# Three norms and the weight blocks behind them, joined without a barrier, in a two-layer diffusion step on one core

## The reference, cut to what matters

```python
for l in range(DEPTH):
    sh1, sc1, gt1, sh2, sc2, gt2 = modulation(cond, w_mod[l], b_mod[l])     # silu(cond) @ w_mod + b_mod
    h = rmsnorm(x, g_pre_mix[l]) * (1.0 + sc1) + sh1
    o = mix(h, ...)                     # u = h @ w_in, attention and RWKV-7, then @ w_o
    x = x + gt1 * rmsnorm(o, g_post_mix[l])
    h = rmsnorm(x, g_pre_ffn[l]) * (1.0 + sc2) + sh2
    f = swiglu(h, w1, w3, w2)           # l == 0; l == 1: top-2 of 8 experts
    x = x + gt2 * rmsnorm(f, g_post_ffn[l])
```

## Time and profile before

| | |
|---|---|
| time, 3 runs | 2856.21 us median (2851.51 to 2856.57) |
| the profiled execution | 2857.58 us, of which span 2855.8 us |
| PE busy | 2631.8 us (92%) |
| DVE busy | 1336.7 us (47%) |
| ACT busy | 1055.3 us (37%) |
| POOL busy | 172.0 us (6%) |
| mean granted clock of TensorE | 0.967 of full |

### The profile page before, as it was taken

How to read it: one execution, slowest core, us unless ns; L and a number is a source line. 1 busy time by engine, 2 the same in 40 slices (tenths; PEclk the granted TensorE clock), 3 DMA queues, 4 the chain that set the end, 5 groups by cost and what they waited for, 6 DMA issues and landing times.

```text
span 2855.8 us, 63857 instructions
## 1 busy us (share of the span) xinstructions
PE 2631.8 (92%) x28250; PEld 2263.3 (79%) x28250; DVE 1336.7 (47%) x2420; ACT 1055.3 (37%) x1993; POOL 172.0 (6%) x175
## 2 busy tenths in 40 slices
PE   5998799997999999999997999979799999999995
PEld 3996588785799994449964878957799999999994
DVE  2237445556422320023464455663456555655565
ACT  3225443444412110023254444442444444444442
POOL 0002011110000000010010111100100000000010
PEclk8999899998999999999998999998899999999998
DMA  6223023300122221121200330001556665666571
GB/s 254 79 76 120 24 99 121 112 12 5 67 74 75 81 74 59 60 77 62 79 18 1 120 103 21 4 5 60 202 186 203 210 211 177 214 207 208 184 263 56
DMA packets 82683, 304.31 MB, mean 107 GB/s; under 512 B 9376, under 2 KB 9504, under 8 KB 82272
## 3 DMA queue, kind: packets, MB, share of 16 engines
q1 hardware_dynamic: 71072, 257.93, 26.4%
q0 software_dynamic: 11328, 42.21, 4.0%
HBM read 273.10 MB, written 27.00 MB: 105 GB/s over the span
## 4 chain that ended last, share of the span: by engine, by line
PE 85%; DVE 9%; ACT 2%; issue 2%; DMA 1%; POOL 0%; DVEq 0%; SPq 0%; PEldq 0%; POOLq 0%; ACTq 0%
PE ps L416 17%; PE ps L417 17%; PE ps L418 17%; PE ps L1303 7%; PE ps L1094 6%; PE ps L1102 3%; PE ps L429 2%; PE ps L744 2%; PE ps L830 2%; PE ps L873 1%; PE ps L1005 1%; PE ps L889 1%; DVE arena L2165 1%; DVE arena L2164 1%; DMA ring<-in_blocks 1%
## 5 line engine op out<-in xcount | busy, mean ns | idle before, releaser
L1987 DVE TENSOR_TENSOR ring_lo<-ring,w_ffn 128x1024 fp32r<-128x1024 f32 x308 | 374.3, 1224 | 215.9 <-ACT w_ffn L1513 210.0
L416 PE MATMUL ps<-hg_hi,w_ffn 128*128 128x256 f32 x1408 | 401.6, 285 | 0.9 <-DVE hg_lo L2505 0.9
L417 PE MATMUL ps<-hg_lo,w_ffn 128*128 128x256 f32 x1408 | 397.2, 282 | 0.0
L418 PE MATMUL ps<-hg_hi,ring_lo 128*128 128x256 f32 x1408 | 396.7, 282 | 0.0
L1513 ACT ACTIVATE w_ffn<-ring 128x1024 fp32r<-128x1024 f32 x308 | 322.3, 1056 | 198.1 <-PE ps L418 197.2
L416 PEld LDWEIGHTS ps<-hg_hi,w_ffn 128*128 128x128 f32 x1408 | 266.5, 189 | 2.6 <-DVE hg_lo L2505 1.1
L417 PEld LDWEIGHTS ps<-hg_lo,w_ffn 128*128 128x128 f32 x1408 | 265.6, 189 | 1.2
L418 PEld LDWEIGHTS ps<-hg_hi,ring_lo 128*128 128x128 f32 x1408 | 266.2, 189 | 0.0
L416 PE MATMUL ps<-hT_hi,w_proj 128*128 128x320 f32 x672 | 211.2, 314 | 8.9 <-DVE hT_lo L1993 8.9
L417 PE MATMUL ps<-hT_lo,w_ffn 128*128 128x320 f32 x704 | 218.2, 310 | 0.0
L416 PE MATMUL ps<-hT_ffn_hi,w_ffn 128*128 128x320 f32 x704 | 213.8, 304 | 4.4 <-DVE hT_lo L1993 4.4
(11 more groups left out here) (350 smaller groups left out, 4807.1 us busy)
## 6 DMA issues: line engine op xcount, KB each, us to landing
ring<-in_blocks SPq DMA_DIRECT2D x484, 512.0 KB, 3.4
h_rows<-arena POOLq DMA_DIRECT2D x16, 512.0 KB, 10.0
arena<-h_rows POOLq DMA_DIRECT2D x7, 1024.0 KB, 10.4
y_rows<-arena POOLq DMA_DIRECT2D x7, 1024.0 KB, 6.6
x<-in_x_all SPq DMA_DIRECT2D x1, 2560.0 KB, 12.9
h_plain<-arena POOLq DMA_DIRECT2D x1, 2560.0 KB, 11.5
out_y_all<-x POOLq DMA_DIRECT2D x5, 512.0 KB, 2.9
w<-in_low POOLq DMA_DIRECT2D x2, 768.0 KB, 4.8
```

Source lines behind the costliest of these rows:

```text
L416: nc.tensor.matmul(dst, w_hi, m_hi, start=start, stop=False)
L417: nc.tensor.matmul(dst, w_hi, m_lo, start=False, stop=False)
L418: return nc.tensor.matmul(dst, w_lo, m_hi, start=False, stop=stop)
L1987: V.tensor_tensor(ring_lo[:, n % RING, :], ring[:, n % RING, :], high[:, n % high.shape[1], :], ALU.subtract).then_inc(*E.sig("w_lo"))
```

## The change

- The sums of squares of norm 0, its scale and its `xn` are made at the head of the modulation: ScalarE's five squares stand ahead of its first `modrow` copy and wait for `x`; VectorE's multiplies stand ahead of its first bias.
- The barriers between modulation and norm 0, between norms 0 and 2 and the projection, and between norm 1 and the dense mixer are gone. At norm 3 nothing changes.
- For norms 0, 1 and 2, turns, scale and shift, split, and the product with the first weight block become one loop over the eight chunks: TensorE turns chunk `kc` and then multiplies chunk `kc - 2` (`norm_into`). ScalarE and VectorE scale chunk `kc` and then split chunk `kc - 1` (`norm_split`). The turns use three pairs of banks, since the product fills pair 0.
- The first weight blocks are split earlier: for the projection two of them ahead of the chunks, for the dense mixer block 0 by ScalarE during the last tile of `wo` and block 1 behind it, into a buffer of their own, `w_first`. VectorE makes both low parts ahead of its first chunk. `w_proj` has moved out of the way of `xn`.
- GpSimd's four loads of layer 0 follow its power of norm 0 as before, but that now stands within the modulation.
- The down product waits for the last but one tile of hidden values at its first matmul, and for the last at its fifth.

```diff
         w_wo = take_r("w_wo", WO_B * D, b=WO_B, d=D)
         vec0 = take(D)
-        assert cursor[0] <= O_AT
+        w_first = take_r("w_first", 2 * D, b=2, d=D)
...
+        cursor[0] = FO_END + NT * D
+        w_proj = take_r("w_proj", 2 * D, b=2, d=D)
...
+        def turn_pair(k, kc):
+
+            return kc % 4 if k == 3 else 1 + (kc + int(k == 0)) % 3
...
+            def norm_turn(k, kc):
+
+                if kc == 0:
+                    pe.wait_ge(sem["norm_x"], NT * (k + 1))
+                if k == 0 and kc == 2:
+                    pe.wait_ge(sem["mod_ev"], MOD_FIRST)
+                if k == 1 and kc in (1, 2):
+                    pe.wait_ge(sem["vec_in"], vec_before(0) + 2 + kc)
+                ahead = 4 if k == 3 else 3
+                if kc >= ahead:
+                    pe.wait_ge(sem["norm_ev_act"], KC * k + kc - ahead + 1)
+                    pe.wait_ge(sem["norm_ev_dve"], KC * k + kc - ahead + 1)
+                for i in range(NT):
+                    mm = nc.tensor.transpose(pair640(turn_pair(k, kc))[:, i * P:(i + 1) * P], xn[:, i, kc * P:(kc + 1) * P], ident)
+                mm.then_inc(sem["norm_tr"], 1)
...
+            def norm_into(k, first, w_h, hi):
+
+                for kc in range(KC + 2):
+                    if kc < KC:
+                        norm_turn(k, kc)
+                    j = kc - 2
+                    if j >= 0:
+                        if j == 0:
+                            w_l = first_split()
+                        pe.wait_ge(sem["x_lo"], first + j + 1)
+                        at = slice(j * P, (j + 1) * P)
+                        mm = mm640_split(nc, 0, w_h[:, at], w_l[:, at], hi[:, j, :], hT_lo[:, j, :], j == 0, j == KC - 1)
+                done(mm)
...
             def proj_phase(l):
-                for o in range(PROJ_B):
+                norm_into(2 * l, X_PROJ[l], w_proj[:, used[0] % 2, :], hT_hi)
+                for o in range(1, PROJ_B):
...
             def dense_phase(l):
...
+                norm_into(2 * l + 1, X_FFN[l], ffn_high(used[0]), hT_ffn_hi)
+                for n in range(1, 2 * FT):
...
-                pe.wait_ge(sem["ff_g"], FT)
                 for h in range(2):
...
                             for i in range(NT):
+                                if h == 0 and f == 0 and i in (0, 4):
+                                    pe.wait_ge(sem["ff_g"], FT - 1 if i == 0 else FT)
...
             for l in range(DEPTH):
                 if l == 0:
                     mod_phase()
-                    next_phase()
-                norm_phase(2 * l)
-                next_phase()
                 proj_phase(l)
...
+            def norm_split(k, high):
+
+                for kc in range(KC + 1):
+                    if kc < KC:
+                        norm_out(k, kc)
+                    if kc >= 1:
+                        act.wait_ge(sem["norm_ev_act"], KC * k + kc)
+                        act.wait_ge(sem["norm_ev_dve"], KC * k + kc)
+                        A(high[:, kc - 1, :], hT[:, kc - 1, :], ACT.Copy).then_inc(*E.sig("x_hi"))
 
             def proj_phase(l):
                 first = PROJ_AT[l]
                 w_hi(w_proj, first)
-                for kc in range(KC):
-                    A(hT_hi[:, kc, :], hT[:, kc, :], ACT.Copy).then_inc(*E.sig("x_hi"))
                 w_hi(w_proj, first + 1)
+                norm_split(2 * l, hT_hi)
...
+                    if l == 0 and i == NT - 1:
+                        w_first_hi(FFN_AT[0])
...
+                    w_first_hi(FFN_AT[0] + 1)
+                    norm_split(2 * l + 1, hT_ffn_hi)
...
+                    norm_start()
                     for m in range(MOD_FIRST):
                         mod_row(m, m)
-                    next_phase()
-                if l == 0:
-                    norm_phase(2 * l)
-                    next_phase()
...
+            def norm_split(k, high):
+
+                for kc in range(KC + 1):
+                    if kc < KC:
+                        norm_out(k, kc)
+                    if kc >= 1:
+                        x_lo(hT_lo[:, kc - 1, :], hT[:, kc - 1, :], high[:, kc - 1, :])
...
             pool.wait_ge(sem["consts_in"], 16)
             for l in range(DEPTH):
                 if l == 0:
-                    next_phase()
                     norm_phase(2 * l)
```

More of the change, by code:

```diff
@@ L765, in norm_phase @@
             def norm_phase(k):
                 for kc in range(KC):
-                    if kc == 0:
-                        pe.wait_ge(sem["norm_x"], NT * (k + 1))
-                    if k == 1 and kc == 2:
-                        pe.wait_ge(sem["vec_in"], vec_before(0) + 4)
-                    if kc >= 4:
-                        pe.wait_ge(sem["norm_ev_act"], KC * k + kc - 3)
-                        pe.wait_ge(sem["norm_ev_dve"], KC * k + kc - 3)
-                    for i in range(NT):
-                        mm = nc.tensor.transpose(pair640(kc % 4)[:, i * P:(i + 1) * P], xn[:, i, kc * P:(kc + 1) * P], ident)
@@ L1793, in dense_phase @@
                 first = FFN_AT[l]
-                w_hi(w_ffn, first)
-                for kc in range(KC):
-                    A(hT_ffn_hi[:, kc, :], hT[:, kc, :], ACT.Copy).then_inc(*E.sig("x_hi"))
-                for n in (1, 2):
-                    w_hi(w_ffn, first + n)
+                w_hi(w_ffn, first + 2)
                 for f in range(FT):
@@ L2056, in proj_phase @@
                 w_lo(w_proj, first)
-                for kc in range(KC):
-                    x_lo(hT_lo[:, kc, :], hT[:, kc, :], hT_hi[:, kc, :])
                 w_lo(w_proj, first + 1)
+                norm_split(2 * l, hT_hi)
                 for o in range(PROJ_B):
@@ L2774, in _ @@
                     continue
+                next_phase()
                 next_phase()
```

119 lines of the change are left out of this document (59 added, 60 removed).

## The result

The changed kernel took 2836.82 us (median of 4 executions, 2834.03 to 2838.43), the kernel before 2856.34 us (median of 4, 2851.51 to 2856.57). The ratio is 0.9935, 95% interval 0.9917 to 0.9952. That is 19.5 us faster, where I forecast 10.2 us (2846.0) and a range down to 2838. The direction was right, the size was not. The profiled execution took 2834.03 us with a span of 2832.2, and TensorE's mean granted clock was 0.971 (0.967 before).

What follows compares the result with a forecast made beforehand. The prediction took TensorE, with 85% of the chain, as the bound, so only its stops could give time. Terms 10.2 - 1.0 + 1.9 + 1.7 less 2.6 for low clock gave 10.2 us: 2856.2 to 2846.0 us, range 2838 to 2854.

Steps and rivals of the forecast that it cites:

- norm 0: Start to first projection block's end: 70.17 becomes 59.95, gain 10.2 us; bracket 6.7 us more or less.
- norm 1: First dense mixer block: `xn` stays at 763.35, block ends at 782.15 against 781.14, a loss of 1.0 us.
- norm 2: Layer 1's first projection block: weight copies lie beside the multiply, end 1296.5 against 1298.42, gain 1.9 us.
- down product: Start of the down product: four matmuls run inside the 2.50 us wait, gain 1.7 us.
- low clock in the loops: Loops of norms 0, 1 and 2: same low-clock stretches as before, 2.6 us a chunk there, 2.6 us lost.
- The first four matmuls of 190.8 / 440 = 0.434 us: Down product: each early matmul priced at 0.434 us, so four gain 1.7 us.
- Behind each, the list of every engine is as before: After the four edited places (norms 0, 1, 2, down product): nothing else changes; their ends are the whole sum.
- collision: End of the modulation: GpSimd's four loads push weight block 15 back by 3.5 us, bounds 0 and 3.96.
- The loop: Norms 0, 1, 2: bound by the way through three engines, 2.05 us a chunk, 13.6 us from first product to block end.
- Half clock through the loop: Rival, loops of three norms: clock stays at half, 4.2 us each; 0.2 us gained, 2856 us, chance 0.13.
- Quicker loop, smaller collision: Rival: loads cost 0.5 us, hops 0.1 us, half the low clock; gain 16.3 us, 2840 us, chance 0.22.
- Slower: Rival: clock falls again behind each of three loops, 6.1 us of product at half clock; 2865 us, chance 0.04.

Runs made afterwards that it cites:

- e4: The changed kernel run again with no edit, as base for the others: 2838.15 us, ratio 0.9947 to the kernel before.
- e7: The kernel before with only `w_proj` put at the changed kernel's place (`vT` moves too): 2849.99 us, ratio 0.9989 to the kernel before.
- e6: The changed kernel with `w_proj` 8 floats further on and nothing else moved: 2842.60 us, ratio 0.9963 to the kernel before.
- e3: The kernel before with only norm 0's squares, scale and `xn` in the modulation, barriers kept, GpSimd's loads behind the first barrier: 2845.01 us, ratio 0.9968.
- e5: The changed kernel with GpSimd's four loads of layer 0 held back until norm 0's turns are done: 2831.58 us, ratio 0.9926 to the kernel before.
- e8: The changed kernel with TensorE multiplying chunk `kc - 3`, not `kc - 2`, behind the turns of chunk `kc`: 2825.32 us, ratio 0.9899 to the kernel before.
- e10: The changed kernel with loads behind norm 0's turns, product three chunks behind, second weight block's low part after the loop: 2820.37 us, ratio 0.9880.

## Why the prediction was wrong in its size

By its own steps, gains in us. The measured gains are by block ends in the profiles where both kernels have them, otherwise by landmarks.

| step | forecast | measured |
|---|---|---|
| norm 0 | 10.2 | 7.6 |
| norm 1 | -1.0 | -1.4 |
| norm 2 | 1.9 | 2.7 (e4, with the long low clock: 0.6) |
| down product | 1.7 | 4.4 (2.7 where the clock holds) |
| `w_proj` at another place | 0 | 4.2 (2.1 in each layer) |
| low clock in the loops | -2.6 | -4.0 (e4: -5.0), inside the norms' rows |
| sum | 10.2 | 17.5 (with e4's norm 2: 15.4) |

The low clock is an estimate: the loops' lengths less 13.2 us each, the length of a loop at full clock. The sum measured fits the 16.1 us of e4 and stands 2 to 4 us under the 19.5 of the first comparison. No step explains that difference; the interval of that comparison's ratio spans 13.7 to 23.7 us.

**"The first four matmuls of 190.8 / 440 = 0.434 us".** This step failed. The row has 440 entries, but the loop has 22 blocks by 2 tiles by 5 token tiles, 220 matmuls: one fp32 matmul of 512 columns stands as two entries. Four matmuls are 8 x 0.434 = 3.5 us, longer than the idle 2.50 us, so all of it goes: 2.7 us measured at an unbroken clock, where I had 1.7. The count in the code would have told it.

**The clock behind the down product's wait.** I left it out, and asked for the clock only at the norms. In the 3.6 us behind that wait the trace of before shows 0.62. The other 1.7 of the 4.4 us are that, in the executions where it happens (three profiles of five). I had cut the gain to what the four matmuls fill, and never asked what ran slow behind the wait.

**"Behind each, the list of every engine is as before".** I took the rest of each list as unchanged in time because it was unchanged in order. The change also moved `w_proj` in memory, and that is worth 2.1 us in each projection (e7, e6). It was an edit of the diff that got no line in the sum, nor a bound. A bound was in the trace of before: the hi*hi pass took 311 ns from `w_proj` and 303 from `w_ffn`, so an address could be worth 8 ns for each of the 16 such matmuls of a block, 2.6 us over 20 blocks.

**Norm 0: collision 3.5, measured 5.6.** The size of the shift was right (3.7). What failed is that I took the shift as the whole cost. It also cut the modulation's end into pieces and let the clock fall ahead of the turns, for 1.9 us more in this pair. By parts, from single profiles of e3 and e5: statistics in the modulation 10.9, the pipeline in place of two barriers 2.3 (59.28 to 56.98), the collision -5.6, together 7.6.

**The loop.** The first product starts 4.58 us behind the end of `xn` at norm 1 (754.68 - 750.10) and at norm 2 (1266.21 - 1261.63), where I had 5.2 and 5.0. The loops lasted 15.7, 14.7 and 13.2 us, where I had 13.6 and some clock. At full clock it is 13.2 us in six loops, against 13.6: the way through three engines was priced right. The low clock was priced too small, 2.6 us for the three loops against 4.0 here and 5.0 in e4. e8 shows the way as the bound, and e10 shows what is left without it. The bracket behind norm 0's gain adds up wrongly: 3.5 and 3.5 us more are 7.0, not 6.7.

**The rivals.** *Half clock through the loop* is out: in the profile of the change the clock was at 0.98 to 1.00 over the last 9 to 10 us of each loop. Beside it stood the Trainium skill (TensorE: Matmul & The Clock Gate, Part 4: PE-mode transpose), by which transposes don't count as busy for the clock. Here again the clock rose from 0.50 to 1.00 between 1261.70 and 1264.90, where TensorE did nothing but 15 transposes, and by that rule it would have stayed low for the first product. That product took 0.38 us, the time of full clock. But in e4 it stayed at 0.50 through the same 15 and beyond, and the first product took 0.61 us. So a rise during transposes alone does occur (before, after, e5 and e6, at norm 2), and what decides it isn't shown. *Quicker loop, smaller collision* gave 2840 and came nearest in time, by luck: the collision was larger, and the loop about as slow as forecast. *Slower* didn't come.

**The range.** The 8 us below the forecast held a quicker loop and a smaller collision only. The clock behind the down product's wait and the new address of `w_proj` had no part in it.

## What to carry to other kernels

- Count the instructions in the code against the entries of a row before a mean is taken as the price of one. A wait's price is its idle time and, in some executions, a low clock behind it: here 1.7 us more behind 2.50, in three profiles of five.
- Where a loop waits for the way through several engines, more work between the first step and the last takes the wait away. One chunk more of distance was worth 2.7 us a loop here, 8 us in all (12.8 by the medians of e4 and e8), and it takes one edit to vary.
- The same loop took 13.2 us at full clock and up to 15.7 where the clock was low for a part of it. Where there are profiles of many runs, sort them by the clock before an edit gets the credit.
- Loads that are moved beside a saturated stream pushed its end back by nearly their full length (3.3 to 3.7 of 3.96 us), and in some executions what waited for that end then ran at a low clock far into the loop (the change and e4, not e6). Here they were put at 26 us when nothing needed them before the attention.

## What the runs showed of the hardware that I had not expected

- Where an operand lies in memory changes how fast TensorE works through it: the hi*hi pass of 128x320 took 311 ns at one place and 303 at another, and 8 floats of shift turned the one into the other. Rounding the address to 16 or 32 floats in the old region gave 310 and 308 and no time. Every place at 303 is a multiple of 128 floats from the start of the shared memory (30080, and 26240 of `w_ffn`). It is worth 2.1 us in each projection.
- The same 2.50 us wait ahead of the down product was followed by a granted clock of 0.60 to 0.64 over 3.6 us in three profiles, and by 1.00 in two.
- One untouched stretch (attention and RWKV of layer 0) took 474.1 to 481.1 us over the profiles, the same loop with the same late block ended at 59.82 or 62.60 us by when the clock came back, and whole executions of the kernel before lay between 2847.99 and 2860.97 us. A pair of single profiles can't tell 5 us apart in this kernel.
